# The ring of weight slots moved by 32 bytes in every partition, the rest by 64

## The reference

```python
def swiglu(h, w_in, w_out):
    a, b = jnp.split(h @ w_in, 2, axis=-1)
    return (jax.nn.silu(a) * b) @ w_out          # w_in: 1024 x 5632, w_out: 2816 x 1024

h = h + 0.5 * swiglu(rmsnorm(h, ffn_norm[layer, 0]), ffn_w_in[layer, 0], ffn_w_out[layer, 0])
...
proj = h @ w_in                                  # mlstm, kv, nsa, fox, dsa
...
return (h_out * jax.nn.sigmoid(og)) @ w_out      # each mixer's way back
```

## Time and profile before

| | |
|---|---|
| median of 3 runs | 1312.43 us (1310.21 to 1314.57) |
| profiled execution, first to last instruction | 1310.3 us |
| PE busy | 1270.2 us (97%), 6717 matmuls |
| VectorE busy | 873.9 us (67%) |
| ScalarE busy | 613.6 us (47%) |
| DMA, the ring's queue | 212.56 MB, 51.2% of 16 engines' time |

### The profile page before, as it was taken

The page is one execution under the profiler, slowest core; times in us unless marked ns, Lnnn a source line. Parts: engine busy times, 40 slices in busy tenths (PEclk is TensorE's granted clock), DMA queues, the critical chain, the costliest instruction groups (busy, mean ns, idle before and its releaser), DMA issues.

```text
span 1310.3 us, 16491 instructions
## 1 busy us (share of the span) xinstructions
PE 1270.2 (97%) x6717; PEld 1077.6 (82%) x6717; DVE 873.9 (67%) x1312; ACT 613.6 (47%) x839; POOL 24.2 (2%) x37
## 2 busy tenths in 40 slices
PE   6999999989999999999999999999999999999997
PEld 5888888988788888878888886778888899988876
DVE  6655557885755556685657569856555567566896
ACT  6444346435434445444435357654444344544461
POOL 2000000100000000000000000000000000000000
PEclk9999999999999999999999989999999999999999
DMA  9655545443555556565665440065666686446401
GB/s 329 207 182 187 186 162 185 142 155 129 183 184 185 188 192 186 166 193 170 217 224 169 159 161 1 1 200 187 191 193 193 130 217 172 150 130 211 176 2 65
DMA packets 158812, 218.17 MB, mean 167 GB/s; under 512 B 8257, under 2 KB 110993, under 8 KB 158737
## 3 DMA queue, kind: packets, MB, share of 16 engines
q1 hardware_dynamic: 156880, 212.56, 51.2%
q0 software_dynamic: 1376, 3.71, 0.9%
q10 hardware_dynamic: 480, 0.85, 0.2%
HBM read 216.04 MB, written 1.05 MB: 166 GB/s over the span
## 4 chain that ended last, share of the span: by engine, by line
PE 82%; DVE 11%; issue 3%; ACT 2%; SPq 1%; DMA 1%; DVEq 0%
PE PS L686 23%; PE PS L689 23%; PE PS L687 23%; DVE wlo L2050 2%; PE PS L823 1%; PE PS L721 1%; PE PS L722 1%; ACT whi L1523 1%; PE PS L706 1%; PE PS L1300 1%; DVE arena L2639 1%; PE PS L728 1%; PE PS L1016 1%; SPq L591 1%; DVE XL L2090 1%
## 5 line engine op out<-in xcount | busy, mean ns | idle before, releaser
L2050 DVE TENSOR_TENSOR wlo<-raw,whi 128x2048 fp32r<-128x2048 f32 (+4 forms) x206 | 457.4, 2230 | 122.6 <-ACT whi L1523 121.8
L1523 ACT ACTIVATE whi<-raw 128x2048 fp32r<-128x2048 f32 (+4 forms) x206 | 381.4, 1863 | 63.4 <-DMA raw<-in_fox_w_in_dram 33.1
L686 PE MATMUL PS<-whi,XL 128*128 128x512 f32 (+3 forms) x992 | 385.8, 390 | 8.9 <-DVE scr L2152 3.8
L687 PE MATMUL PS<-wlo,XH 128*128 128x512 f32 (+3 forms) x992 | 379.8, 384 | 0.0
L689 PE MATMUL PS<-whi,XH 128*128 128x512 f32 (+3 forms) x992 | 265.0, 384 | 0.0
L686 PEld LDWEIGHTS PS<-whi,XL 128*128 128x128 f32 x992 | 187.3, 189 | 45.1 <-DVE scr L2152 4.9
L689 PEld LDWEIGHTS PS<-whi,XH 128*128 128x128 f32 x992 | 185.5, 190 | 35.5
L687 PEld LDWEIGHTS PS<-wlo,XH 128*128 128x128 f32 x992 | 187.4, 189 | 32.9
L1577 ACT ACTIVATE scr<-PS,rn 128x256 f32<-128x256 f32 x88 | 41.7, 474 | 225.2 <-PE PS L689 223.9
L686 PE MATMUL PS<-whi,GL 128*128 128x512 f32 x320 | 125.4, 392 | 0.0
L687 PE MATMUL PS<-wlo,GH 128*128 128x512 f32 x320 | 124.6, 389 | 0.0
(11 more groups left out here) (387 smaller groups left out, 1339.2 us busy)
## 6 DMA issues: line engine op xcount, KB each, us to landing
raw<-in_ffn_w_in_dram SPq DMA_DIRECT2D x174, 512.0 KB, 5.0
raw<-in_ffn_w_out_dram SPq DMA_DIRECT2D x88, 512.0 KB, 4.9
raw<-in_fox_w_in_dram SPq DMA_DIRECT2D x24, 512.0 KB, 7.9
raw<-in_a_w_in_dram SPq DMA_DIRECT2D x16, 512.0 KB, 4.6
raw<-in_dsa_w_in_dram SPq DMA_DIRECT2D x16, 512.0 KB, 6.0
raw<-in_kv_w_dram SPq DMA_DIRECT2D x12, 512.0 KB, 4.2
raw<-in_fox_w_in_dram SPq DMA_DIRECT2D x12, 344.0 KB, 5.0
raw<-in_a_w_out_dram SPq DMA_DIRECT2D x8, 512.0 KB, 4.9
```

What stands on the lines that cost most here:

```text
L686: mm(o, xl, wh, start=start and i == 0, stop=False, skip_group_check=True)
L687: mm(o, xh, wl, start=False, stop=False, skip_group_check=True)
L1523: A(whi[:, p % SLOTS, 0:n], raw[:, p % SLOTS, 0:n], ACT.Copy).then_inc(hi_done, 1)
L2050: V.tensor_tensor(wlo[:, p % SLOTS, 0:n], raw[:, p % SLOTS, 0:n], whi[:, p % SLOTS, 0:n].bitcast(F32), ALU.subtract).then_inc(lo_done, 1)
```

## The change

It creates two tensors that nothing reads or writes, 8 f32 in each partition: one ahead of `whi`, one behind `wlo`.

```diff
+        sb("half_line", [P, 8])
         whi = sb("whi", [P, SLOTS, PIECE], F32R)
         lo_at = (nc.sbuf_base + 31) // 32 * 32
         wlo = sb("wlo", [P, SLOTS, PIECE], F32R)
         raw = nc.alloc_sbuf_tensor_at("raw", [P, SLOTS, PIECE], F32, offset=lo_at)
+        sb("half_line_after", [P, 8])
         h = sb("h", [P, NT, D])
```

## The result

The changed kernel takes 1330.84 us against 1313.33 us for the kernel before (medians of four runs each): a ratio of 1.0141, with a 95% interval from 1.0127 to 1.0155. It is slower by 1.4% (the two medians alone are 17.5 us apart, 1.3%), where 10.1 us, 0.8%, was forecast. The profiled execution spans 1329.0 us for 1310.3, 18.7 us more, at the same granted clock, 0.992 in both.

A forecast was written before the change was run, and what follows sets the result against it. TensorE's start-to-start matmul distances were taken to bound the kernel: 13.1 - 3.2 + 0.3 + 0.2 + 1.0 = +11.4 us on TensorE, 0.89 of it on the path, so 1312.4 + 10.1 = 1322.5 us; range 1298 to 1333, the forecast's own 1317 to 1328.

The forecast's parts named there:

- What bounds the kernel: Whole program: TensorE busy 97% of the span; time is the number of matmuls times their start-to-start distance.
- 512 columns moving: 3984 products streaming 512-column weight rows, now begun at byte 32: +3.3 ns each, +13.1 us; bounds -3.3 to +6.6 ns.
- lines: TensorE's operand reads: a 64-byte line touched in part costs its full 16 columns, 6.7 ns.
- Ring stationary: 960 products with weights as stationary operand and XH or XL moving: 120.0 becomes 116.7 ns, -3.3 each, -3.2 us.
- 384 columns: 3 x 32 products of 384 columns: 25 lines and 10.0 make 176.7 ns, +2.9 each, +0.3 us.
- 272: 48 products of 272 columns: 18 lines, 130.0 ns, +5.0 each, +0.2 us.
- FL and FH: 96 products with FL and FH stationary: both operands at 32, 17 lines, 126.6 ns, +9.9 each, +1.0 us.
- 344 and 372 columns: Products of 344 and 372 columns: as many lines touched as before, change 0.
- Splits and transfers: ScalarE's copy and VectorE's subtraction into the ring, and DMA into it: taken as 0, with 3.5 us kept in the range.
- Slower by twice as much: Rival on TensorE: 33 lines and the dearer remainder stays, +6.6 ns on 4080 rows, 25 us on the path, 1338; chance 0.09.
- Faster, places alone count: Rival on TensorE: only operands' difference of place counts, partly touched lines are free; -14.6 us on the path, 1298; chance 0.24.
- No change: Rival on TensorE: 64-byte lines do not exist for its reads, 512 columns keep 226.7 ns; 1309.6 to 1312.4 us; chance 0.21.

The follow-up runs named there:

- rows372: Bare f32r products without the model, rows of 372, 344, 272 columns packed or at one distance; 372 columns: packed 169.6 ns, 169.9 at distance 0, 166.7 at 32 and 64.
- ahead_only: Kernel before plus only the 32 unused bytes ahead of the weight ring, so weights and activations both move by 32: 1314.17 us against 1311.91, ratio 1.0007.

## Why the prediction was right in its sign and wrong in its size and its mechanism

*What bounds the kernel* held. The time followed the distances: over all products of 512 columns behind which PE did not wait (distances under 260 ns), the mean went from 227.5 to 233.2 ns, 5.7 x 3984 = 22.7 us. (It grew by less than the 6.6 ns of a steady run because part of the products took more than 226.7 before.) Over the 1056 products of 256 columns with the ring, FL and FH among them, the mean of the distances under 130 ns went from 119.6 to 117.2, -2.5. The sum of +20.2 on PE became 18.7 us of span, a share of 0.93 where the prediction put 0.89.

*512 columns moving* is the step that failed, and with it the size: +3.3 ns were taken, the trace has +6.6, the upper bound of that step, and so the time lies above the forecast's own range of 1317 to 1328. In place of lines the runs show the distance between the two operands: for these products it went from 0 to 224 modulo 256 bytes, and the table has 226.7 and 233.2 ns there. The prediction chose by the rows of 372 and 344 columns, because they were the only moving rows that begin off a line. But these rows lie at several distances from their stationary blocks at once, so they could not show what one distance does, and rows372 shows that no line is needed for them. The choice of the nearest row was a choice by a property, place in a line, that does not matter. The prediction had named this sign itself: it is wrong at its root if the remainder of 372 columns has a cause other than lines. So the sign of the forecast was right by luck: the dearer 512 columns that gave it are there, but not for the reason that was given.

*Ring stationary*, -3.3 ns: right in size (116.7). Its reason, that operands at different places are cheaper, is true for 256 columns at a distance of 32 and false for 512, which pay 6.6 for the same difference. *384 columns* were put at +2.9 and did not move, *272* at +5.0 and stayed at 125.0; neither pays for a line. *FL and FH* were put at 126.6 and came to 119.7: the dearer remainder was right (their distance went from 32 to 0), the seventeenth line was not there. *344 and 372 columns* did not change, as predicted, but the reason given, as many lines as before, falls with the lines. For 344 columns rows372 shows that no distance it tried matters by more than 1.8 ns; why 372 columns held still was not shown. *Splits and transfers* at 0: right, with 2289 and 1910 ns, and ScalarE idle 57.0 us for 57.5.

*The rivals.* "Slower by twice as much" had the right 6.6 ns, on the 512 columns alone. Its mechanism was 33 lines and a remainder that stays dear, and ahead_only refutes that: with both operands off the line it would be 1337 us, and is 1314. "Faster, places alone count" had the right idea, that the two operands' places count only against each other, with the sign of the 256 columns. "No change" was right that lines of 64 bytes explain nothing here, and the rule of the Trainium skill beside it ("SBUF — State Buffer", specifications) agrees so far: a shift of both operands by 32 cost nothing in the whole kernel and in bare products of 512, 384 and 256 columns (those of 448 took 4.0 ns more). That this leaves the time alone did not follow, since the shift also changes the distance.

The rule of the Trainium skill that was weighed, on the page "TensorE: Matmul & The Clock Gate", separate read ports for the moving operand and the weights (its part on what happens when a matmul is issued), would make the place of the stationary operand indifferent. The runs disagree: with the moving rows at 0, the stationary block's move from 0 to 32 alone took 512 columns from 226.7 to 233.2 ns. That does not say that the ports are shared, only that the time of a product depends on both places together.

## What to carry to other kernels

In a kernel in which TensorE is hardly ever idle, count the distances from one start to the next, and look at how moving and stationary operands lie to each other modulo 256 bytes before a buffer is put between them: an allocation of 32 or 64 bytes between weights and activations cost 1.4 to 1.5% here, and the same bytes ahead of both cost nothing that could be measured. For f32r products of 512 columns that all lie alike, with starts at multiples of 32, keep the distance at a multiple of 256. And where a rule is read from rows of one trace, make it foretell a case in which its terms come apart before the large term is hung on it; here a bare loop of 48 products for each case did this, and the whole kernel then followed it.

## What the runs showed of the hardware

That the cost of a product depends on the distance between its operands, with a period of 256 bytes, was not expected. For 512 columns 226.7 ns at 0 and 228.9 to 234.2 elsewhere; for 256 columns 120.0 at 0 and 117.7 to 119.8 elsewhere; for 384 columns 173.3 at 0, 32 and 64 and 176.1 at 128. The values of 256, 384 and 512 columns at 0 are 16, 24 and 32 times 6.67 ns (16 columns at 2.4 GHz) plus two such units, 13.3; most of the dear ones of 512 columns are near three units, 20.0. A narrower stationary block does not shorten the 226.7, and shortens the 233.3 of a distance of 32 by some 2 ns at most. Which of the neighbouring blocks a moving row meets, why rows of 384 columns are spared at 32 and 64, and why 448 columns differ at one and the same distance, was not settled.
